# Eleven projection units with x's high and low parts side by side under the high weights, and the low sums added afterwards

## The reference

```python
proj = hn @ w_in                                        # hn 256 x 1024, w_in 1024 x 4112
qkv = jax.nn.silu(causal_depthwise_conv(proj[..., :3 * DN_DIM], conv_w))   # 3 x 1024 columns, 4 taps
# q, k: l2norm over each head of 128; then beta, g and the chunked recurrence over q, k, v
```

## Time and profile before

| what | value |
|---|---|
| three runs | 1269.4 us median, 1269.24 to 1269.87 |
| the profiled execution, its own time | 1266.35 us |
| its span in the profile | 1264.6 us |
| PE, DVE, ACT busy | 97%, 69%, 55% of the span |
| chain that ended last | PE 80%, DVE 10%, ACT 4%, DMA 2% |
| units 1 to 11 on PE | 20.88 us to 88.3 us |

### The profile page before, as it was taken

How to read it: one execution, slowest core, us unless ns; L and a number is a source line. 1 busy time by engine, 2 the same in 40 slices (tenths; PEclk the granted TensorE clock), 3 DMA queues, 4 the chain that set the end, 5 groups by cost and what they waited for, 6 DMA issues and landing times.

```text
span 1264.6 us, 21628 instructions
## 1 busy us (share of the span) xinstructions
PE 1230.9 (97%) x8628; PEld 1115.2 (88%) x8628; DVE 874.9 (69%) x1266; ACT 700.8 (55%) x1025; POOL 62.8 (5%) x101
## 2 busy tenths in 40 slices
PE   8999989999999999999999999999999999999997
PEld 7998988888889997888888999899999987888886
DVE  5887567566566656666567499998655566878775
ACT  5984565455555545555555545556454355666663
POOL 4020021000000001000000000010000010000000
PEclk9999999999999999999999999999999999999999
DMA  7671134655664544556663764544556542555551
GB/s 225 190 200 68 37 132 149 219 199 199 199 197 153 182 153 134 183 200 198 199 200 100 233 194 141 151 150 134 177 163 189 188 142 75 185 198 200 184 183 65
DMA packets 160340, 210.80 MB, mean 167 GB/s; under 512 B 5542, under 2 KB 143220, under 8 KB 160261
## 3 DMA queue, kind: packets, MB, share of 16 engines
q1 hardware_dynamic: 157315, 202.77, 49.9%
q0 software_dynamic: 1904, 6.85, 1.4%
q10 hardware_dynamic: 1042, 0.07, 0.1%
HBM read 208.62 MB, written 1.05 MB: 166 GB/s over the span
## 4 chain that ended last, share of the span: by engine, by line
PE 80%; DVE 10%; ACT 4%; DMA 2%; issue 2%; SPq 1%; POOL 0%; DVEq 0%; POOLq 0%; ACTq 0%
PE bank L367 17%; PE bank L371 17%; PE bank L370 17%; PE bank L435 15%; PE bank L431 8%; DVE wlo L303 3%; PE bank L1340 1%; ACT whi L295 1%; DMA raw<-in_dn_w_in 1%; ACT common L672 1%; PE bank L1360 1%; SPq L3209 1%; PE bank L1895 1%; DVE common L2435 1%; PE bank L2022 1%
## 5 line engine op out<-in xcount | busy, mean ns | idle before, releaser
L303 DVE TENSOR_TENSOR wlo<-raw,whi 128x2048 fp32r<-128x2048 f32 x190 | 434.5, 2289 | 201.4 <-ACT whi L295 201.0
L295 ACT ACTIVATE whi<-raw 128x2048 fp32r<-128x2048 f32 x190 | 362.9, 1912 | 147.5 <-PE bank L367 44.3
L367 PE MATMUL bank<-xparts,whi 128*128 128x256 f32 x944 | 272.6, 289 | 3.7 <-DVE xparts L749 3.3
L370 PE MATMUL bank<-xparts,whi 128*128 128x256 f32 x944 | 267.7, 284 | 0.0
L371 PE MATMUL bank<-xparts,wlo 128*128 128x256 f32 x944 | 267.6, 283 | 0.0
L435 PE MATMUL bank<-xparts,whi 128*128 128x512 f32 x864 | 216.4, 392 | 0.0
L367 PEld LDWEIGHTS bank<-xparts,whi 128*128 128x128 f32 x944 | 181.7, 192 | 7.1 <-issue 5.4
L370 PEld LDWEIGHTS bank<-xparts,whi 128*128 128x128 f32 x944 | 181.7, 192 | 1.1 <-issue 1.0
L371 PEld LDWEIGHTS bank<-xparts,wlo 128*128 128x128 f32 x944 | 181.6, 192 | 0.0
L435 PEld LDWEIGHTS bank<-xparts,whi 128*128 128x128 f32 x864 | 155.4, 189 | 27.8
L367 PE MATMUL bank<-whi,hhi 128*128 128x512 f32 x392 | 153.1, 390 | 5.7 <-DVE hlo L2976 2.9
(11 more groups left out here) (361 smaller groups left out, 1660.6 us busy)
## 6 DMA issues: line engine op xcount, KB each, us to landing
raw<-in_mlp_w_up SPq DMA_DIRECT2D x32, 1024.0 KB, 5.5
raw<-in_mlp_w_down SPq DMA_DIRECT2D x32, 1024.0 KB, 5.0
raw<-in_w_in SPq DMA_DIRECT2D x22, 1024.0 KB, 5.2
raw<-in_w_up SPq DMA_DIRECT2D x22, 1024.0 KB, 5.1
raw<-in_w_gate SPq DMA_DIRECT2D x16, 1024.0 KB, 5.5
raw<-in_dn_w_in SPq DMA_DIRECT2D x15, 1024.0 KB, 6.0
raw<-in_mb_w_in SPq DMA_DIRECT2D x12, 1024.0 KB, 5.1
raw<-in_w_down SPq DMA_DIRECT2D x11, 1024.0 KB, 4.9
```

The lines of the kernel that those rows point to most:

```text
L295: nc.scalar.activation(whi[:, s, :], raw[:, r, :], ACT.Copy).then_inc(hi_ready, 1)
L303: nc.vector.tensor_tensor(wlo[:, s, :], raw[:, V % RAW, :], f32(whi[:, s, :]), ALU.subtract).then_inc(lo_ready, 1)
L367: ins = pe.matmul(o, shi, mhi, start=first, stop=False, skip_group_check=True)
L370: pe.matmul(o, shi, mlo, start=False, stop=False, skip_group_check=True)
```

## The change

Unit 0 stays as it is. Units 1 to 11 use `wide_features` with two banks each: odd units G2 and G3, even units G0 and G1. ACT copies the low halves into `cin`, 512 columns of the `masks` tile that is not yet in use (`copy_low`), DVE adds the main halves to them there (`add_low`, which frees the banks), and all four taps read `cin`. A new semaphore, `dn_tapped`, says that the taps of a unit are done; `finish_unit` waits for it.

```diff
-            uses = [G[u % 4].use() for u in range(12)]
+            uses = [[G[0].use()]] + [[G[2 * (u % 2) + f].use() for f in range(2)] for u in range(1, 12)]
+            low = [None] + [low_sum.many(2) for u in range(1, 12)]
+            tapped = Signal(sem("dn_tapped")).many(12)
+            cin = masks[:, 0:512]
...
-                        gemm_features(pe, units[u], uses[u], xhi, xlo)
+                        wide_features(pe, units[u], uses[u])
...
-                act.wait_ge(uses[u].freed, uses[u].n + 1)
+                act.wait_ge(tapped[u].sem, tapped[u].value)
...
-                    act.wait_ge(uses[u].filled, uses[u].n + 1)
+                    if u:
+                        copy_low(act, cin, uses[u], low[u])
+                        for use in uses[u]:
+                            act.wait_ge(use.freed, use.n + 1)
+                    else:
+                        act.wait_ge(uses[0][0].filled, uses[0][0].n + 1)
+                    src = cin if u else uses[0][0].ps
...
                 for u in range(12):
+                    if u:
+                        add_low(dve, cin, uses[u], low[u])
                     split_lo(dve, units[u])
+                    src = cin if u else uses[0][0].ps
...
-                                qkv[:, ft, sh:T], uses[u].ps[:, f * T:(f + 1) * T - sh],
+                                qkv[:, ft, sh:T], src[:, f * T:(f + 1) * T - sh],
                                 convw[:, j, ft:ft + 1], qkv[:, ft, sh:T], ALU.mult, ALU.add)
                             if j == 0 and f == 1:
-                                ins.then_inc(uses[u].freed, 1)
+                                ins.then_inc(tapped[u].sem, 1)
...
+                    if u == 0:
+                        dve.wait_ge(tapped[0].sem, tapped[0].value)
+                        dve.sem_inc(uses[0][0].freed, 1)
```

More of the change, by code:

```diff
@@ L1121, in pe_in @@
                     if u == 0:
-                        first_product(pe, uses[0], norm)
+                        first_product(pe, uses[0][0], norm)
                     else:
-                        gemm_features(pe, units[u], uses[u], xhi, xlo)
+                        wide_features(pe, units[u], uses[u])
                     if u == 0:
@@ L1164, in act_in @@
                         finish_unit(act, u - 1)
-                    act.wait_ge(uses[u].filled, uses[u].n + 1)
+                    if u:
[5 more added lines that the diff above has]
+                    src = cin if u else uses[0][0].ps
                     for f in range(2):
                         ft = 2 * u + f
-                        ins = nc.scalar.activation(qkv[:, ft, :], uses[u].ps[:, f * T:(f + 1) * T], ACT.Copy,
+                        ins = nc.scalar.activation(qkv[:, ft, :], src[:, f * T:(f + 1) * T], ACT.Copy,
                                                    scale=convw[:, 3, ft:ft + 1])
```

## The result

The changed kernel takes 1285.31 us (median of four, 1284.29 to 1287.25) beside 1269.32 us for the kernel before: ratio 1.0134, 95% interval 1.0120 to 1.0148. It is 16.0 us slower, where 12.0 was forecast; the time lies near the upper end of the stated range (1276.5 to 1286). Its profiled execution, 1287.25 us with a span of 1285.2, is the slowest of its four, and that of before (1266.35) was faster than every other one of its kernel, so the two profiles lie 20.6 us apart. The account is therefore made at points inside the stage first.

The account below looks back on a forecast made before the run. The projection was taken as PE-bound before, then bound by a DVE/ACT loop of 6.22 us a turn against PE's 5.59. Turns, table loads and stage end made PE 12.0 us later: 1269.4 + 12.0 = 1281.4 us, range 1276.5 to 1286.

Parts of the forecast that it names:

- So PE follows at 6.22 us: Projection: only two bank sets, so PE cannot outrun the DVE/ACT loop's 6.22 us turn, 0.63 us more than PE's 5.59.
- The wait ahead of unit 2: PE's gap until DVE's taps free unit 0's bank; any clock fall there hidden, since the loop is later anyway.
- Loads of weights: DMAs in the projection: 0.8 us of room, nothing lost unless a load takes more than some 6.7 us.
- the prediction's margin: Hops between engines, 0.04 us each, three a turn, eight turns; at 0 or 0.1 each the sum moves -1 or +1.5.
- t(9): Start of DVE's split behind the adds of unit 9 in the projection, forecast at 88.84 us.
- that rival, 1278.3: Projection taps shorter from SBUF, 2.03 us for six, making a turn 5.83 and the shift 8.9 us; chance 8%.
- The first that PE needs from this side are the keys: Behind the projection: PE needs keys at 108.3 us, ACT has them at 107.4; any excess lateness makes PE wait.
- That hides: Behind the projection: DVE's first matrices come 13.8 us later, 1.8 more than PE, at no cost.
- I take 0: Clock fall to 1.2 GHz behind PE's gap ahead of unit 11: priced at 0, ends 0 and 2 us.
- more than the loop: Rival: clock fall ahead of unit 11 and late keys add 2 us and 1 us, giving 1284.4; chance 14%.

Follow-up runs that it names:

- filler and early means: Changed kernel plus unread matmuls in two PE gaps and DVE's last square means ahead of unit 11's taps: 1281.94 us, ratio 1.0101 to the kernel before.
- the second profile of the change: Profile from timing the changed kernel again, unedited, beside the kernel before: 1284.07 us, ratio 1.0119.
- with it opened: Changed kernel with ACT's SiLU behind the first tap and two buffers for the joined sums: 1281.05 us, ratio 1.0095 to the kernel before.
- the one with filler: Changed kernel plus unread matmuls on PE, 36 ahead of unit 2 and 15 before unit 11's transpose: 1282.92 us, ratio 1.0118 to the kernel before.

## Why the prediction was right, and where it was wrong

**Right: the sign, and the mechanism.** DVE's adds, split and taps, ACT's SiLU and copies, and DVE's adds again form a closed loop that is longer than PE's unit and makes PE late. Its turns came within 0.1 us of the forecast, those with table loads within 0.21 (8.08 and 7.87 for 7.87 and 7.66), and the chain that ended last runs round it. Taking SiLU out (1280.65) makes the kernel faster, and moving the split (1288.70) doesn't, so it is the loop and not the place of the split.

**Not so: "So PE follows at 6.22 us".** PE ran units 3 to 6 at 5.6 us and met the loop again at unit 8. Its waits were 9.7 us and not 13 to 14. The total held all the same, because unit 11 stands behind ACT's copy in iteration 10, whose time the loop sets, however PE gets to it.

**Right: what was costed at nothing.** The wait ahead of unit 2 was hidden (1284.93 without it). The keys did not come late. Loads of weights did not lengthen a turn, though the room was less than the 0.8 us forecast: at 50.89 ACT's split began 1.01 us late by its load and ended some 0.2 us before the taps, for which the SiLU waits.

**Mis-sized: the loop and what follows it, 12.0 forecast, 13.0 measured** (first decays with filler and early means). A turn is 6.29, not 6.22: taps take 2.45 from SBUF, and the hops take a few hundredths more. (The sum holds two hops a turn; the prediction's margin counts three.) In the first profile t(9) is 0.8 us late, and ACT's taps from SBUF, 0.91 for two where they took 0.82, add 0.1. The hop from ACT's copy to PE is 0.15 and not 0.04, and from the transpose to the decays PE takes 7.68 at full clock (94.07 to 101.75) and not 7.46. The Trainium skill (Perfetto Trace Analysis, section Optimizing Scalar/DVE Operations) gives ScalarE some 42 ns more on SBUF than on PSUM, an estimate of 0.08 for two, and the trace agrees with 0.09. The same passage's 65 ns less for VectorE is not seen: six taps went from 2.42 to 2.45, and that rival, 1278.3, falls.

**Wrong: "The first that PE needs from this side are the keys".** It needs something earlier. PE's second Gram product goes into bank O1, and that bank holds the transposed square sums of unit 11's end until DVE's `dve_square_means` has read them, which stands behind the last taps in DVE's queue. The prediction had followed the semaphores of the operands and not who last used each bank. It had even computed that DVE would be 1.8 us later than PE, and costed it at nothing ("That hides"). Measured: a wait of 1.70 us, which cost 2.0 from start to start, and which went when the square means were moved ahead of the taps.

**Wrong: "I take 0" for the clock ahead of unit 11.** The gap of 1.9 us was foreseen, and the price bounded at 2 us; the zero was a choice without a row behind it. The trace before shows both outcomes: behind the gap of 2.19 us ahead of the earlier trace rows the clock was 0.50, behind one of 2.94 us at 1250.58 it was 1.00. Measured in the first profile: 9.23 us from the transpose at 94.33 to the decays, where 7.68 are needed at full clock, so 1.6 us. The rival "more than the loop", 1284.4, had a late DVE and a fallen clock in it, though by the keys and not by the bank; at 14% it was given too little. The fall is not in every execution in this place: in the second profile of the change it came one unit earlier, and the first decays, at 102.92, are 1.2 us later than with filler and early means.

**The account.** At the third decays of the first profile: 12.0 forecast, 1.2 for the turns, ACT's taps, the hop and PE's own 7.68, 1.6 for the clock, 2.0 for the bank: 16.8, as measured. For the whole: the kernel with both extras off measures 13.0, with the bank 15.0, the change 15.2 and 16.0. What is left, 0.2 to 1.0 us, is of the size of the clock's falls, which differ from one execution to the next; it is within the intervals, and how much of it is the clock was not settled.

**What was not foreseen at all** is what lies beneath the loop: with it opened the kernel takes 1281, not the 1272 to 1275 that I expected of that run, since ACT's queue by itself is late by then. The prediction had summed DVE's work for a unit (5.3 us) and not ACT's.

## What to carry to other kernels

When a change adds a hand-over between two engines, write down one turn of the queue orders as a cycle and add it up, before comparing busy times; here engines busy for 55% and 69% of the span held back one at 97%. Then sum each engine's own queue, table loads included, since opening the cycle gives back only what lies above that. For what comes late behind it, follow the banks' last readers as well as the operands. And give a TensorE gap of about 2 us a price and a chance for the clock behind it, not a zero: here it was 1.6 us in one execution and none in that place in another.

## What the runs showed of the hardware

- TensorE's clock went to its lower level, 1.2 GHz (granted clock 0.50 to 0.66 in windows), behind gaps of 4.30, 2.05 and 1.92 us in the first profile of the change and behind one of 2.32 in the second. The length of the gap alone doesn't tell: in the same place, ahead of the square sums, PE waited 2.32 us in the second profile (then 0.50) and 2.31 in the one with filler (then 1.00). The Trainium skill (TensorE: Matmul & The Clock Gate, Part 1) says that the default is the throttled state and activity releases it; the rises agree with that, from 0.50 at 34 to 36 us to 1.00 from 38 us on while PE worked without a pause (first profile), and from 0.50 to 0.92 at 174 to 176 us in the kernel before.
- With 36 and 15 matmuls put into two of the gaps it stayed at 1.00, 2.4 GHz, behind these two. It still fell elsewhere in that profile, behind a wait of 2.25 us (0.64 at 62 to 66 us), and there PE met a later wait for the adds, of 1.46 us, all the same.
- The changed kernel had such falls in different places from one execution to the next, also without a gap of that size: at 160 us in one profile of the change it went to 0.53 straight behind 7 us of small matmuls with PE busy for 6.70 of them, and in the other it stayed at 1.00. The executions of one of these kernels spread by 1.5 to 5.2 us; that the falls make this spread was not shown.
- Taps of 255 columns cost VectorE about the same from SBUF as from PSUM, 2.45 and 2.42 us for six.
